# A recurrent layer in a TensorE stream: outputs placed behind the next group's gates, and the last two in full precision

## The chip, the cores and the metric

The kernel runs on one core of one Trainium2 chip, in one launch. The metric is the device time in microseconds. An execution is a run of the whole program.

## The reference, cut to what matters

The model has four layers on 256 tokens (272 with 16 meta tokens) of width 1024: an attention layer, the recurrent layer with which this case deals, and two layers of FFN, mixer and FFN. The recurrent layer, of width W = 2048:

```python
zp = einsum('btd,de->bte', z, w_in)            # u and gate, W columns each
u, gate = split(zp)
xc = conv_b + sum(up[:, tap:tap + T] * conv_w[tap] for tap in range(4))
def direction(xc, w_a, b_a, w_x, b_x, lam, reverse):
    xb = xc.reshape(B, T, 16, 128)             # 16 blocks of 128 channels
    r = sigmoid(einsum('btnd,nde->btne', xb, w_a) + b_a)
    i = sigmoid(einsum('btnd,nde->btne', xb, w_x) + b_x)
    log_a = -8.0 * r * softplus(-lam)
    a, b = exp(log_a), sqrt(-expm1(2 * log_a)) * i * xc
    return scan(h = a_t * h + b_t, reverse)
y = (direction(forward) + direction(backward)) * silu(gate)
h = h + einsum('bte,ed->btd', y, w_out)
```

All values are float32.

## The kernel before

Activations lie as [128 channels, tile, tokens]. Weights come from one stream in memory, in slabs of 128 x 1024 (512 KB), in the order of use. SyncE (SP) loads them into three buffers `raw`. ScalarE rounds a slab to its high half (`w_hi`, L452), VectorE forms the rest (`w_lo`, L888); this is a split. Both halves have a ring of six, and the splits run `LEAD` = 4 slabs ahead of TensorE. TensorE makes each product of three matmuls (`mm3`, L1431 to L1433): high by high, high weight by low activation, low weight by high activation. So 24 matmuls use up a slab. A matmul on float32 that isn't split is one line in the code and two instructions in the profile.

The recurrent layer takes its 16 blocks of channels in four groups of four. A block n = 4g + r has: an input slab (`u`, eight products of 272 columns, `from_z`); the convolution, a tap on ScalarE (L767) and three on VectorE (L1342); four gate matmuls in full precision (`lru`, L1667), whose weights POOL loads unsplit into two buffers `WL` (L401); four tanh on ScalarE (L780); an input-gate slab of 256 columns and its tanh (L791). ScalarE turns gates into decays (`decay`, L799), `tau` (L809) and, for a whole group after it, `roots` (L815, for the last group L819), with a change of the activation table before and behind. VectorE has `gated` (L1353, L1356), and `scans`: L1363, L1365, the scans L1366 and L1367, L1369, L1371. The result is split by `high` (ScalarE, L827) and `low` (VectorE, L1376) and goes with an output slab into the sums in PSUM banks 0 to 3 (`down`, eight blocks of 256 columns).

PSUM banks 4 to 7 take the tiles `u`, `lru`, `gate` in turn, by their place in `ODD_TILES` modulo 4; a tile waits for the reader of the tile four places before.

The order is written out by hand in each engine's queue. TensorE: inputs of group g, for g of 2 and 3 the output of group g - 2, gates of group g; at the end outputs 2 and 3. VectorE: four convolutions, for g of 2 and 3 four splits and `low` of group g - 2, then for each r a split, `gated` and the scans of group g - 1; at the end, for each r, split, `low` of group 2 and scans of group 3, and four splits with `low` of group 3. ScalarE goes likewise: taps (the decays, tau and roots of the group before between them), output splits and `high`, then per r gates, output gate, `decay` and `tau`. After the layer, `enter` adds the sums to the residual (L922), forms the next normalization's parts, and the first FFN's slabs follow.

## Time and profile before

| what | value |
|---|---|
| time, median of 3 runs | 1720.17 us (1717.52 to 1721.12) |
| the profiled execution's own time | 1717.52 us |
| its span | 1715.7 us |
| TensorE busy | 1598.8 us, 93% |
| VectorE busy | 1153.1 us, 67% |
| ScalarE busy | 912.1 us, 53% |
| granted clock of TensorE, mean | 0.974 of full |
| DMA | 263.67 MB, mean 154 GB/s |

The profile is one execution, times from the start of its span. The recurrent layer's first product starts at 357.98 us, and the first FFN's begins at 589.25. Durations of matmuls overlap: the distance of two starts is what one costs. A granted clock of 1.00 is 2.4 GHz, 0.50 is 1.2 GHz. A row of the timeline gives start, duration, engine, line, operation, tiles, count, and in brackets how long the engine idled before it and which instruction ended that.

### The profile page before, as it was taken

How to read it: one execution, taken by the hardware profiler on the slowest of the kernel's cores; microseconds unless marked ns; L12 is line 12 of the kernel's file. 1: busy time of each engine (PE TensorE's matmuls, PEld its weight loads, DVE VectorE, ACT ScalarE, POOL GpSimd, SP SyncE). 2: the span in 40 equal slices, each digit the busy share in tenths (PEclk: the TensorE clock that was granted, in tenths of full speed). 3: DMA queues.
4: the chain of work that ended last, by engine and by line, in shares of the span. 5: the costliest groups of instructions: out<-in, count | busy, mean ns of one | idle time of the engine just before them, and what ended most of it. 6: DMA issues, size and time to landing. Idle time of an engine off the chain costs nothing.

```text
span 1715.7 us, 32420 instructions
## 1 busy us (share of the span) xinstructions
PE 1598.8 (93%) x12554; PEld 1541.3 (90%) x12554; DVE 1153.1 (67%) x1750; ACT 912.1 (53%) x1432; POOL 44.6 (3%) x52
## 2 busy tenths in 40 slices
PE   7998797988776899999999999999999999999996
PEld 7988675987776899999999999999999899999996
DVE  4546668566686866668777766676666877776666
ACT  5453555457676454447654544455444765454443
POOL 0000000000000000000300000000000030000000
PEclk9999999989998899999999999999999999999998
DMA  5442300533442365554545565546555454546554
GB/s 194 160 159 74 97 1 1 180 126 125 135 148 84 126 203 186 186 183 136 172 148 173 167 199 185 183 159 205 186 185 188 129 175 146 176 166 199 183 183 135
DMA packets 73314, 263.67 MB, mean 154 GB/s; under 512 B 8144, under 2 KB 9680, under 8 KB 73104
## 3 DMA queue, kind: packets, MB, share of 16 engines
q1 hardware_dynamic: 71712, 256.85, 45.8%
q0 software_dynamic: 1520, 5.66, 1.0%
q8 instruction: 59, 0.97, 0.2%
q14 instruction: 23, 0.19, 0.0%
HBM read 261.43 MB, written 1.05 MB: 153 GB/s over the span
## 4 chain that ended last, share of the span: by engine, by line
PE 75%; DVE 15%; ACT 6%; issue 3%; DMA 2%; DVEq 0%; SPq 0%; ACTq 0%
PE PS L1431 22%; PE PS L1433 22%; PE PS L1432 22%; DVE w_lo L888 3%; ACT w_hi L452 1%; PE PS L1754 1%; DMA raw<-stream 1%; DVE zf L1229 1%; PE PS L1608 1%; PE PS L1442 1%; ACT work L809 1%; DVE stat L1284 1%; PE PS L1585 1%; PE PS L1586 1%; DVE zf L1280 1%
## 5 line engine op out<-in xcount | busy, mean ns | idle before, releaser
L1431 PE MATMUL PS<-YH,w_hi 128*128 128x256 f32 (+1 forms) x2876 | 831.9, 289 | 44.4 <-DVE YL L1376 31.7
L1433 PE MATMUL PS<-YH,w_lo 128*128 128x256 f32 (+1 forms) x2876 | 818.3, 285 | 0.0
L1432 PE MATMUL PS<-YL,w_hi 128*128 128x256 f32 (+1 forms) x2876 | 818.2, 285 | 0.0
L888 DVE TENSOR_TENSOR w_lo<-raw,w_hi 128x1024 fp32r<-128x1024 f32 x484 | 594.6, 1232 | 235.8 <-ACT w_hi L452 232.8
L1431 PEld LDWEIGHTS PS<-YH,w_hi 128*128 128x128 f32 x2876 | 549.3, 191 | 55.4 <-DVE YL L1376 33.8
L452 ACT ACTIVATE w_hi<-raw 128x1024 fp32r<-128x1024 f32 x484 | 508.2, 1053 | 139.9 <-PE PS L1433 87.1
L1432 PEld LDWEIGHTS PS<-YL,w_hi 128*128 128x128 f32 x2876 | 549.2, 191 | 1.9 <-issue 0.5
L1433 PEld LDWEIGHTS PS<-YH,w_lo 128*128 128x128 f32 x2876 | 550.2, 191 | 0.0
L1431 PE MATMUL PS<-hH,w_hi 128*128 128x256 f32 x832 | 233.0, 280 | 6.4 <-DVE hL L979 6.4
L1432 PE MATMUL PS<-hL,w_hi 128*128 128x256 f32 x832 | 233.0, 280 | 0.0
L1433 PE MATMUL PS<-hH,w_lo 128*128 128x256 f32 x832 | 232.9, 280 | 0.0
L1431 PEld LDWEIGHTS PS<-hH,w_hi 128*128 128x128 f32 x832 | 156.8, 188 | 7.2 <-DVE hL L979 7.2
L1432 PEld LDWEIGHTS PS<-hL,w_hi 128*128 128x128 f32 x832 | 156.5, 188 | 0.0
L1433 PEld LDWEIGHTS PS<-hH,w_lo 128*128 128x128 f32 x832 | 156.3, 188 | 0.0
L972 DVE TENSOR_TENSOR zf<-PS,work 128x256 f32<-128x256 f32 x88 | 37.2, 423 | 171.4 <-PE PS L1433 171.4
L507 ACT ACTIVATE zf<-zf 128x256 f32<-128x256 f32 x88 | 36.8, 418 | 181.7 <-DVE zf L970 181.7
L511 ACT ACTIVATE hH<-zf 128x256 fp32r<-128x256 f32 x88 | 36.6, 416 | 138.6 <-DVE zf L975 138.6
L970 DVE TENSOR_TENSOR zf<-PS,work 128x256 f32<-128x256 f32 x88 | 37.2, 423 | 33.7 <-PE PS L1433 33.7
L641 ACT ACTIVATE work<-PS 128x272 f32<-128x272 f32 (+4 forms) x61 | 23.1, 411 | 46.2 <-PE PS L1433 26.9
L1667 PE MATMUL PS<-work 128*128 128x272 f32 x128 | 35.8, 411 | 9.7 <-DVE work L1356 4.8
L975 DVE TENSOR_TENSOR zf<-zf 128x256 f32<-128x256 f32 x88 | 37.4, 425 | 5.8 <-ACT zf L507 3.3
L1667 PEld LDWEIGHTS PS<-work 128*128 128x128 f32 x128 | 22.5, 192 | 17.6 <-DVE work L1356 8.3
(288 smaller groups left out, 1377.6 us busy)
## 6 DMA issues: line engine op xcount, KB each, us to landing
raw<-stream SPq DMA_DIRECT2D x484, 512.0 KB, 4.0
work<-stream POOLq DMA_DIRECT2D x8, 512.0 KB, 4.2
X<-x SPq DMA_DIRECT2D x1, 1088.0 KB, 5.1
out<-zf SPq DMA_DIRECT2D x8, 128.0 KB, 2.0
work<-rope SPq DMA_DIRECT2D x1, 544.0 KB, 7.6
work<-levels POOLq DMA_DIRECT2D x1, 512.0 KB, 3.9
work<-inv_count POOLq DMA_DIRECT2D x1, 512.0 KB, 4.6
work<-band POOLq DMA_DIRECT2D x1, 408.0 KB, 4.6
```

The source lines that it names most:

```text
L452: act.activation(w_hi[:, s.slot, :], raw[:, s.slot % RAW, :], ACT.Copy).then_inc(hi_ready, 1)
L507: act.activation(sg[:, b, :], sg[:, b, :], ACT.Silu).then_inc(sg_ready, 1)
L511: act.activation(hH[:, b, 0:T2], hf[:, b, :], ACT.Copy).then_inc(hhi_ready, 1)
L641: act.activation(dst, PS[0:rows, 4 + j % 4, 0:width], ACT.Copy).then_inc(job_out, 1)
L888: dve.tensor_tensor(w_lo[:, s.slot, :], raw[:, s.slot % RAW, :], f32(w_hi[:, s.slot, :]), ALU.subtract).then_inc(lo_ready, 1)
L970: dve.tensor_tensor(sg[:, b, :], PS[:, 4 + b, 0:T2], rsb, ALU.mult).then_inc(ga_ready, 1)
L972: dve.tensor_tensor(hf[:, b, :], PS[:, 6 + b, 0:T2], rsb, ALU.mult).then_inc(up_ready, 1)
L975: dve.tensor_tensor(hf[:, b, :], hf[:, b, :], sg[:, b, :], ALU.mult).then_inc(hf_ready, 1)
L1431: pe.matmul(to, wh, xh, start=start, stop=False, skip_group_check=True)
L1432: pe.matmul(to, wh, xl, start=False, stop=False, skip_group_check=True)
L1433: return pe.matmul(to, wl, xh, start=False, stop=stop, skip_group_check=True)
L1667: pe.matmul(tile("lru", n, q), WL[:, n // 2 % 2, k * P:(k + 1) * P], XC[:, g % 2, r, :], start=True, stop=True, skip_group_check=True).the ...
```

## The change

- Output g - 1 is done on TensorE behind the gates of group g, for g of 1 and 2. The outputs of groups 2 and 3 come at the end, from unsplit slabs in full precision (`whole_output`): eight matmuls of 256 columns a slab, from `WL` and `GR` as they are, without `high`, `low` or split.
- POOL loads these eight slabs too. `WL` has four buffers in place of two; a wait on `whole_used` frees them. SP's ring has 40 slabs of this layer and not 48.
- VectorE and ScalarE: the scans of a group are spread over three places: set 0 at the end of the group's own phase (for group 0 behind the next convolutions), sets 1 and 2 among the next gates, set 3 among the output splits. Decay 3, tau 2 and 3 and the roots of groups 1 to 3 move from between the next taps to the end of the group's own phase.
- PSUM: inputs take banks 4 to 7, gate matmuls rotate over 4 to 6, the input gate has 7; a tile waits for the reader of the last tile in its bank.
- `high` and `low` no longer wait for a free buffer: `YH`, `YL` hold groups 0 and 1 in eight places.

```diff
@@ -54,7 +54,7 @@
...
 def o_u(g):
-    return (0, 8, 16, 28)[g]
+    return (0, 8, 20, 32)[g]
@@ -62,31 +62,45 @@
...
 def o_out(g):
-    return (20, 32, 40, 44)[g]
+    return (16, 28)[g]
...
 LRU_SLABS = 8
-O_RING = O_SLABS - LRU_SLABS
+WHOLE_SLABS = LRU_SLABS + 8
+WHOLE = 4
+O_RING = O_SLABS - WHOLE_SLABS
...
-    ring, lru = [0] * O_RING, []
+    ring, lru, out = [0] * O_RING, [], []
     for g in range(GROUPS):
...
             ring[o_gate(g) + r] = (4, 14, 28, 38)[g] + 3 * (r // 2) + r % 2
-            ring[o_out(g) + r] = (24, 44, 48, 52)[g] + r
+            if g < 2:
+                ring[o_out(g) + r] = (24, 44)[g] + r
+            else:
+                out.append((48, 52)[g - 2] + r)
         lru += [(4, 14, 28, 38)[g] + 3 * p + 2 for p in range(2)]
-    return ring, lru
+    return ring, lru + out
...
 for _g in range(GROUPS):
-    ODD_TILES += [("u", 4 * _g + _r, 0) for _r in range(4)]
+    ODD_TILES += [(4 + _r, "u", 4 * _g + _r, 0) for _r in range(4)]
     for _r in range(4):
-        ODD_TILES += [("lru", 4 * _g + _r, _q) for _q in range(4)] + [("gate", 4 * _g + _r, 0)]
+        ODD_TILES += [(4 + (4 * (4 * _g + _r) + _q) % 3, "lru", 4 * _g + _r, _q) for _q in range(4)] + [(7, "gate", 4 * _g + _r, 0)]
+def odd_place(kind, n, q=0):
+    banks = [t[0] for t in ODD_TILES]
+    at = [t[1:] for t in ODD_TILES].index((kind, n, q))
+    older = [i for i in range(at) if banks[i] == banks[at]]
+    return banks[at], ODD_TILES[older[-1]][1:] if older else None
@@ -227,7 +241,7 @@
...
         GR, GS = part(2, 4, T2), part(4, T2)
-        WL = part(2, SLAB)
+        WL = part(WHOLE, SLAB)
         HS = zf[:, 0:2, :]
@@ -272,7 +286,7 @@
...
         sp_d, sp_a = sem("sp_d"), sem("sp_a")
-        lru_landed = [sem(f"lru_landed{i}") for i in range(2)]
+        whole_landed, whole_used = [sem(f"whole_landed{i}") for i in range(WHOLE)], sem("whole_used")
         tap_done, xc_ready, lru_done, lru_out = sem("tap_done"), sem("xc_ready"), sem("lru_done"), sem("lru_out")
@@ -328,14 +342,12 @@
...
-        RING_SOURCE, LRU_SOURCE = odd_source()
+        RING_SOURCE, WHOLE_SOURCE = odd_source()
         def odd_bank(kind, n, q=0):
-            return 4 + ODD_TILES.index((kind, n, q)) % 4
+            return odd_place(kind, n, q)[0]
         J_KS, J_QS, J_VS, J_Q, J_K, J_V, J_G, J_ODD = 6, 8, 16, 19, 31, 39, 45, 61
         UNITS = [("pe", 0), ("sk", 0)] + [(kind, j) for j in range(4) for kind in ("mq", "mk", "sq")]
@@ -357,18 +369,19 @@
...
                 sp.dma_start(m, mats[:, i, :]).then_inc(c_loaded, 16)
-            for n in range(RAW, E_SLABS + O_RING):
+            first = -(-(E_SLABS + O_RING) // RAW)
+            for n in range(RAW, first * RAW):
                 sp.wait_ge(lo_ready, n - RAW + 1)
-                source = n if n < E_SLABS else E_SLABS + RING_SOURCE[n - E_SLABS]
+                source = n if n < E_SLABS else E_SLABS + RING_SOURCE[n - E_SLABS] if n < E_SLABS + O_RING else n + WHOLE_SLABS
                 sp.dma_start(raw[:, n % RAW, :], stream[source]).then_inc(landed[n % RAW], 16)
-            with sp.Fori((E_SLABS + O_RING) // RAW, (slabs - LRU_SLABS) // RAW) as turn:
+            with sp.Fori(first, (slabs - WHOLE_SLABS) // RAW) as turn:
                 for s in range(RAW):
...
                     sp.wait_ge(lo_ready, turn * RAW + s - RAW + 1)
-                    sp.dma_start(raw[:, s, :], stream[turn * RAW + s + LRU_SLABS]).then_inc(landed[s], 16)
-            for n in range((slabs - LRU_SLABS) // RAW * RAW, slabs - LRU_SLABS):
+                    sp.dma_start(raw[:, s, :], stream[turn * RAW + s + WHOLE_SLABS]).then_inc(landed[s], 16)
+            for n in range((slabs - WHOLE_SLABS) // RAW * RAW, slabs - WHOLE_SLABS):
                 sp.wait_ge(lo_ready, n - RAW + 1)
-                sp.dma_start(raw[:, n % RAW, :], stream[n + LRU_SLABS]).then_inc(landed[n % RAW], 16)
+                sp.dma_start(raw[:, n % RAW, :], stream[n + WHOLE_SLABS]).then_inc(landed[n % RAW], 16)
             for c in range(DC):
@@ -394,11 +407,13 @@
...
             pool.wait_ge(x_ready, 4)
-            for i in range(LRU_SLABS):
-                if i >= 2:
-                    pool.wait_ge(lru_done, 8 * (i - 1))
-                pool.dma_start(WL[:, i % 2, :], stream[E_SLABS + LRU_SOURCE[i]]).then_inc(lru_landed[i % 2], 16)
+            for i in range(WHOLE_SLABS):
+                if i >= WHOLE + LRU_SLABS:
+                    pool.wait_ge(whole_used, i - WHOLE - LRU_SLABS + 1)
+                elif i >= WHOLE:
+                    pool.wait_ge(lru_done, 8 * (i - WHOLE + 1))
+                pool.dma_start(WL[:, i % WHOLE, :], stream[E_SLABS + WHOLE_SOURCE[i]]).then_inc(whole_landed[i % WHOLE], 16)
@@ -821,41 +836,41 @@
...
                     act.wait_ge(oy_ready, n + 1)
-                    if g >= 2:
-                        act.wait_ge(w_used, odd(o_out(g - 2) + r).n + 1)
-                    act.activation(YH[:, 8 + n % 8, 0:T2], GR[:, g % 2, r, :], ACT.Copy).then_inc(oyhi_ready, 1)
+                    act.activation(YH[:, 8 + n, 0:T2], GR[:, g % 2, r, :], ACT.Copy).then_inc(oyhi_ready, 1)
...
                         tap(g, r)
-                        if g and r == 0:
-                            decay(g - 1, 3)
-                            tau(g - 1, 2)
-                            tau(g - 1, 3)
-                        if g and r == 1:
-                            roots(g - 1)
-                    if g >= 2:
-                        for r in range(4):
-                            split(odd(o_out(g - 2) + r + LEAD))
-                            high(g - 2, r)
+                        if g == 1 and r == 0:
+                            decay(0, 3)
+                            tau(0, 2)
+                            tau(0, 3)
+                        if g == 1 and r == 1:
+                            roots(0)
                     for r in range(4):
...
                             decay(g, r - 1)
-                            if r > 1:
-                                tau(g, r - 2)
-                decay(LAST, 3)
-                tau(LAST, 2)
-                tau(LAST, 3)
-                roots(LAST)
-                for r in range(4):
-                    split(odd(o_out(LAST - 1) + r + LEAD))
-                    high(LAST - 1, r)
-                for r in range(4):
-                    split(odd(o_out(LAST) + r + LEAD))
-                    high(LAST, r)
+                        if r > 1:
+                            tau(g, r - 2)
+                            if 0 < g < LAST:
+                                high(g - 1, r - 2)
+                    if g:
+                        if g < LAST:
+                            split(odd(o_out(g - 1) + LEAD))
+                        decay(g, 3)
+                        tau(g, 2)
+                        if g < LAST:
+                            split(odd(o_out(g - 1) + 1 + LEAD))
+                        tau(g, 3)
+                        if g < LAST:
+                            high(g - 1, 2)
+                            split(odd(o_out(g - 1) + 2 + LEAD))
+                            high(g - 1, 3)
+                        roots(g)
+                        if g < LAST:
+                            split(odd(o_out(g - 1) + 3 + LEAD))
@@ -916,6 +931,8 @@
...
                     dve.wait_ge(sums_ready, 3 * n + j + 1)
+                elif s is None:
+                    dve.wait_ge(whole_used, WHOLE_SLABS - LRU_SLABS)
                 else:
@@ -1373,28 +1390,33 @@
...
                     dve.wait_ge(oyhi_ready, n + 1)
-                    dve.tensor_tensor(YL[:, 8 + n % 8, 0:T2], GR[:, g % 2, r, :], f32(YH[:, 8 + n % 8, 0:T2]),
+                    dve.tensor_tensor(YL[:, 8 + n, 0:T2], GR[:, g % 2, r, :], f32(YH[:, 8 + n, 0:T2]),
                                       ALU.subtract).then_inc(oylo_ready, 1)
...
                         conv(g, r)
-                    if g >= 2:
-                        for r in range(4):
-                            split(odd(o_out(g - 2) + r + LEAD))
-                            low(g - 2, r)
+                    if g == 1:
+                        scans(0, 0)
                     for r in range(4):
...
                         gated(g, r)
-                        if g:
+                        if g and r in (1, 2):
                             scans(g - 1, r)
+                    if 0 < g < LAST:
+                        low(g - 1, 0)
+                        low(g - 1, 1)
+                        split(odd(o_out(g - 1) + LEAD))
+                        scans(g - 1, 3)
+                        split(odd(o_out(g - 1) + 1 + LEAD))
+                        low(g - 1, 2)
+                        split(odd(o_out(g - 1) + 2 + LEAD))
+                        low(g - 1, 3)
+                        split(odd(o_out(g - 1) + 3 + LEAD))
+                        scans(g, 0)
+                scans(LAST - 1, 3)
                 for r in range(4):
-                    split(odd(o_out(LAST - 1) + r + LEAD))
-                    low(LAST - 1, r)
                     scans(LAST, r)
-                for r in range(4):
-                    split(odd(o_out(LAST) + r + LEAD))
-                    low(LAST, r)
@@ -1407,7 +1429,7 @@
...
             for lay in range(LAYERS):
-                enter(lay * 3, lay * 3 + 1, layer_slab(lay, -1), 0.5, lay * C_LAYER + C2 + C_F1)
+                enter(lay * 3, lay * 3 + 1, layer_slab(lay, -1) if lay else None, 0.5, lay * C_LAYER + C2 + C_F1)
                 ffn(layer_slab(lay, K_FFN[0]), lay * 2 * FF, lay * 3)
@@ -1636,39 +1658,54 @@
...
-                    at = ODD_TILES.index((kind, n, q))
-                    if at >= 4:
-                        was, m, k = ODD_TILES[at - 4]
+                    bank, older = odd_place(kind, n, q)
+                    if older:
+                        was, m, k = older
                         if was == "u":
...
                             pe.wait_ge(lru_out, 4 * m + k + 1)
-                    return PS[:, odd_bank(kind, n, q), 0:width]
+                    return PS[:, bank, 0:width]
...
                         pe.wait_ge(oylo_ready, n + 1)
-                        down(odd(o_out(g) + r), YH[:, 8 + n % 8, 0:T2], YL[:, 8 + n % 8, 0:T2], n == 0, n == 15)
+                        down(odd(o_out(g) + r), YH[:, 8 + n, 0:T2], YL[:, 8 + n, 0:T2], n == 0, False)
+                def whole_output(g):
+                    for r in range(4):
+                        n = 4 * g + r
+                        i = LRU_SLABS + n - 8
+                        pe.wait_ge(whole_landed[i % WHOLE], 16 * (i // WHOLE + 1))
+                        pe.wait_ge(oy_ready, n + 1)
+                        for m in range(DC):
+                            last = pe.matmul(PS[:, m // 2, (m % 2) * T2:(m % 2 + 1) * T2], WL[:, i % WHOLE, m * P:(m + 1) * P],
+                                             GR[:, g % 2, r, :], start=False, stop=n == 15, skip_group_check=True)
+                            if n == 15 and m in (1, 3, 5):
+                                last.then_inc(sums_ready, 1)
+                        last.then_inc(whole_used, 1)
...
                         from_z(odd(o_u(g) + r), tile("u", 4 * g + r), 1 if g == r == 0 else None, T1)
-                    if g >= 2:
-                        output(g - 2)
                     for r in range(4):
                         n = 4 * g + r
-                        pe.wait_ge(lru_landed[n // 2 % 2], 16 * (n // 4 + 1))
+                        i = n // 2
+                        pe.wait_ge(whole_landed[i % WHOLE], 16 * (i // WHOLE + 1))
                         pe.wait_ge(xc_ready, n + 1)
...
                             k = 4 * (r % 2) + q
-                            pe.matmul(tile("lru", n, q), WL[:, n // 2 % 2, k * P:(k + 1) * P], XC[:, g % 2, r, :],
+                            pe.matmul(tile("lru", n, q), WL[:, i % WHOLE, k * P:(k + 1) * P], XC[:, g % 2, r, :],
                                       start=True, stop=True, skip_group_check=True).then_inc(lru_done, 1)
                         from_z(odd(o_gate(g) + r), tile("gate", n, 0, T2), None, T2, XO)
-                output(LAST - 1)
-                output(LAST)
+                    if 0 < g < LAST:
+                        output(g - 1)
+                whole_output(LAST - 1)
+                whole_output(LAST)
 
```

## Rows read from the trace of the kernel before

**Rows 1.** Windows by stage: us, busy (instructions) per engine, clock, DMA, GB/s.

```profile
412.90:469.40 56.50, 46.83 (x322) 43.72 (x320) 39.27 (x60) 34.94 (x58) 1.06 (x2) 0.91 0.41 134
469.40:524.30 54.90, 45.00 (x320) 41.82 (x320) 39.17 (x60) 35.56 (x60) 1.05 (x2) 0.94 0.42 135
524.30:589.20 64.90, 46.75 (x312) 43.34 (x312) 50.54 (x80) 34.87 (x63) 0.00 (x0) 0.84 0.30 98
```

**Rows 2.** List of waits, 358 to 589 us: total, times, longest.

```profile
PE PS L1431 <- DVE YL L1376: 31.7, 6, 11.7
...
PE PS L1667 <- DVE work L1356: 4.8, 6, 0.9
```

**Rows 3.** Timeline of TensorE: start, duration, instruction, idle before and releaser.

```profile
453.67 0.58 PE L1431 MATMUL PS<-YH,w_hi 128*128 128x256 f32 x1 [7.67 <-DVE YL L1376]
...
479.51 0.72 PE L1667 MATMUL PS<-work 128*128 128x272 f32 x2 [0.83 <-DVE work L1356]
...
555.56 0.58 PE L1431 MATMUL PS<-YH,w_hi 128*128 128x256 f32 x1 [11.66 <-DVE YL L1376]
...
565.80 0.39 PE L1431 MATMUL PS<-YH,w_hi 128*128 128x256 f32 x1 [2.03 <-DVE YL L1376]
```

**Rows 4.** Timeline of TensorE without waits: gate pair, then four input slabs.

```profile
378.38 2.00 PE L1667 MATMUL PS<-work 128*128 128x272 f32 x8
380.01 0.48 PE L1431 MATMUL PS<-YH,w_hi 128*128 128x256 f32 x1
...
383.02 1.99 PE L1667 MATMUL PS<-work 128*128 128x272 f32 x8
...
488.85 0.29 PE L1431 MATMUL PS<-YH,w_hi 128*128 128x272 f32 x1
...
500.83 0.29 PE L1433 MATMUL PS<-YH,w_lo 128*128 128x272 f32 x1
```

**Rows 5.** Timeline of VectorE: one scan set, a split and the gating.

```profile
473.62 0.72 DVE L1363 SCALAR_TENSOR_TENSOR work<-work 128x544 f32<-128x544 f32 x1
...
477.27 1.22 DVE L888 TENSOR_TENSOR w_lo<-raw,w_hi 128x1024 fp32r<-128x1024 f32 x1
478.41 0.72 DVE L1353 SCALAR_TENSOR_TENSOR work<-work 128x544 f32<-128x544 f32 x1
479.04 0.41 DVE L1356 SCALAR_TENSOR_TENSOR work<-work,PS 128x256 f32<-128x256 f32 x1
```

**Rows 6.** Timeline of ScalarE: tap, table load, root; output gate, decay, tau.

```profile
401.79 0.58 ACT L767 ACTIVATE work<-PS,C 128x272 f32<-128x272 f32 x1
402.39 1.28 ACT L815 ACT_TABLE_LOAD   x1
403.68 2.02 ACT L815 ACTIVATE work<-work 128x2176 f32<-128x2176 f32 x1
...
483.08 0.38 ACT L791 ACTIVATE work<-PS 128x256 f32<-128x256 f32 x1 [1.37 <-PE PS L1433]
483.36 1.11 ACT L799 ACTIVATE work<-work,sp 128x272 f32<-128x272 f32 x2
484.37 1.11 ACT L809 ACTIVATE work<-work,sp 128x272 f32<-128x272 f32 x2
```

**Rows 7.** Windows of one microsecond, columns as in the first group.

```profile
413.00:414.00 1.00, 1.00 (x6) 0.88 (x5) 0.00 (x0) 0.44 (x2) 0.00 (x0) 0.50 0.36 143
...
567.00:568.00 1.00, 1.00 (x7) 1.00 (x6) 0.97 (x3) 0.00 (x0) 0.00 (x0) 0.50 0.84 336
...
570.00:571.00 1.00, 0.50 (x5) 0.29 (x3) 1.00 (x3) 0.47 (x1) 0.00 (x0) 0.99 0.00 0
```

**Rows 8.** Timeline of TensorE at the fourth gate matmul of tile 4.

```profile
412.25 1.27 PE L1667 MATMUL PS<-work 128*128 128x272 f32 x2 [1.50 <-DVE work L1342]
```

**Rows 9.** Timeline of ScalarE: the four roots of group 3.

```profile
550.67 2.29 ACT L819 ACTIVATE work<-work 128x544 f32<-128x544 f32 x4
```

**Rows 10.** DMA issues: count, KB each, median us from issue to landing.

```profile
work<-stream POOLq DMA_DIRECT2D x8, 512.0 KB, 4.2
```

## The prediction

> **What bounds the kernel now.** I read the windows by stage first. In the recurrent layer TensorE works 46.8 of 56.5 us, 45.0 of 54.9 and 46.8 of 64.9 in three stretches, at a granted clock of 0.84 to 0.94 of full; in the last VectorE is busier, 50.5 [rows 1]. The reader sees there a layer in which no engine is full. The list of waits says who ends TensorE's idle time: the low half of a gated output (L1376), 31.7 us in six waits of matmuls, 11.7 the longest (and about as much again put on weight loads); 4.8 us are put on VectorE's L1356 [rows 2]. TensorE's timeline gives the places: 7.67 us before output 0 (and as much again before output 1), 11.66 before output 2, then 2.03 inside the last eight output slabs (and 2.12 once more), and 0.83 before a fourth gate matmul, of which there are five alike [rows 3]. So the layer is bound by order: outputs stand where their inputs are not ready, and in the tail each slab waits for its scans, a split and a low half on VectorE.
>
> **Unit costs.** One pair of gates and input gate goes from 378.38 to 383.02, 4.64 us without a wait [rows 4]. Of these the split slab (24 matmuls of 256 columns) has 383.02 less 380.01, 3.01, of which 0.18 is still the matmul before (the pitch of the rest is 0.118): 2.83. The four full-precision matmuls of 272 columns are then 1.81, 0.453 each; at 256 columns 0.426, so an output slab of eight in full precision is 3.41 us. An input slab: 95 pitches in 11.98 us [rows 4], 0.126 each, 3.03. VectorE: a scan set goes from 473.62 to 477.27, 3.65 us; a split's pitch is 1.14, the first gating operation's 0.63; the second has 0.41 less the 0.08 by which these rows overlap, 0.33, and a low half of the same shape is taken at 0.34 [rows 5]. ScalarE: output gate 0.28 by pitch, decay 1.01 for two instructions (tau, of the same shape, as much, and a gate tanh 0.5), a tap 0.58, a table load 1.28 [rows 6].
>
> **The change, part by part.** I take TensorE's work from the gate of tile 4 on (before it the order is as now) and add the waits that the other two queues leave. A group's cycle (gates, output of the group before, inputs of the next) is 4 x 4.64 + 4 x 2.83 + 4 x 3.03 = 42.0 us. The waits:
> - *Banks.* Gates rotate over three banks, the input gate has the fourth. The fourth gate matmul no longer waits for L1356 of the tile before, but for ScalarE's first tanh of its own tile. In the third tile that stands behind output gate and decay (0.28 + 1.01 + 0.5 and 0.2 for hand-overs, less the 1.36 of three matmuls: 0.65); in the fourth behind tau and a high half too (1.0 + 0.3 more: 1.9); in the first behind the last tap and the table load (0.58 + 1.28 + 0.5, less 1.36: 1.0). Bounds for the three together: nothing, where VectorE is late anyway, to 5.
> - *Output behind the gates.* The first low half follows the last gating: 1.2 us after the gates. The third slab's low half is queued on VectorE behind two low halves, a split that waits for ScalarE's high half, a scan set and another split. From the gates' end: 3.7 to the first of these splits' start, then 1.14 + 3.65 + 1.14 + 0.34 = 10.0 us; the first wait and two slabs take 1.2 + 5.66. So 3.2 us. Bounds: 0, since [rows 3] has slabs that follow without a wait, and 7.67, the wait of now.
> - *Scans.* Sets 1 and 2 lie beside the gates, 3 between the output's splits, 0 at the end of it. VectorE's sum for a cycle is 4 x (1.14 + 1.60) for convolutions, 4 x 3.65, 4 x (1.14 + 0.96), 4 x 1.48 for the output: 39.9 us. It is under 42.0 and doesn't become the bound, by only 2.
> - *Clock.* After the wait of 2.03 us the clock is at 0.50 in the slice from 567 and at 0.99 in that from 570 [rows 7]: 3 us or a little more at half speed; I take 1.7 us lost. I saw no such fall after the waits of 0.83. So I charge the 3.2 us wait 1.8 and each 1.9 us wait half of 1.7. At tile 4 the clock is at 0.50 [rows 7] and stays so: 1.8, in place of the 1.1 us by which the gating would be late there (scan set 0 of group 0 is put ahead of it).
>
> Group 1, gate 4 to gate 8: 42.0 + 0.65 + 1.9 + 1.0 + 1.2 + 3.2 + 1.8 + 1.8 = 53.5; now it is the first stretch of [rows 1], 56.5. Group 2, without the slow start: 51.7; now 54.9, the second stretch. Gate 4 starts at 412.25 and not 0.68 later: now the fourth gate matmul waits till then for the fourth convolution [rows 8], after only the gate does. Together 6.9 us won.
>
> - *The tail.* Group 3's gates cost about what they do now (3 more pairs, and 0.65 + 1.9 for the waits of 0.83 and the like): now TensorE idles from 555.56 less 11.66, 543.90 [rows 3], and a matmul's row reaches 0.16 beyond its pitch, so they end at 543.7; the last stretch ends with the layer at 589.2 [rows 1]: 45.5 us. After, eight slabs of 3.41 are 27.3: TensorE has 8 x 0.58 = 4.7 us more work than with split slabs, VectorE and ScalarE lose eight splits and halves. Let T be the gates' end. Output 2's last set is done at T + 4.5 and used at T + 10.2. For group 3 ScalarE has decay, tau, decay, tau, tau, a load and a first root, as now, where the first of the four roots ends 0.6 after 550.67 [rows 9]: T + 7.6. Sets end at T + 11.2, 14.9, 18.5, 22.2; the slabs want them at T + 13.6, 17.1, 20.5, 23.9. With 1.7 us to spare they are hidden; were this cover gone, each us of delay beyond it costs one. The tail can't be under 22.2 + 3.4 = 25.6. Won: 18.2.
> - *DMAs.* POOL issues eight slabs of 512 KB more, SP eight less. A slab lands in 4.2 us [rows 10]; with four buffers one comes free three slabs, 10.2 us, ahead of its use, so it is hidden; a landing of 12 us would cost 2 for each of the last four. The two loads that now go first have nothing waiting behind them. levels and inv_count stand behind the last slab on POOL, but wait for the layer's end anyway.
> - *Hand-over to the FFN.* It is VectorE's own chain from the second column pair on; the last slab's extra 0.58 is in the 27.3.
>
> Sum: 6.9 + 18.2 less 3 x 0.85 is 22.6, say 23 us. The profiled execution took 1717.52 around a span of 1715.7, so 1694.5 for one like it. The median of the runs is 1720.17, 2.65 above it: I forecast 1697.
>
> **A rule weighed.** On ScalarE the switch to square roots took 1.28 us, 402.39 to 403.67, and the next instruction began at 403.68 [rows 6]. The Trainium skill (ScalarE: Activation LUTs, What ACT_TABLE_LOAD costs) says that a switch also drains for some 1.38 us. By that, an estimate from its figure, two cycles would be 1.4 us dearer each and the sum 20. The trace doesn't agree for this switch, so the sum goes by the row.
>
> **Rivals.**
> 1. *Only the tail pays.* The third slab's wait is near 7 us, because its low half sits behind a scan set and ScalarE's chain per tile is longer. For it: VectorE has only 2 us to spare in a cycle. Against: it also loses no time there to the 7 us stalls that it has now. Won 18.2 less up to 2: 1703. Chance 0.13.
> 2. *Shorter waits, no clock loss.* 2 x 1.8, 2.6 and a part of the tanh waits come back: 1689. For it: 0.83 us waits cost no clock. Chance 0.10.
> 3. *Slower: the clock doesn't come back.* Four waits now follow each other within 20 us. If after them the clock stayed at 0.50 through the output and the first input slab (14.4 us of work, doubled, less the 1.8 counted: 12.6) in two cycles, and through half of the full-precision stretch (13.7), it would cost 38.9 against 22.6: 1736. It decides from some 23 us of work at 0.50 on, beyond what is counted. For it: the low clock around tile 4. Against: after the 2.03 us wait it was back within 4 us [rows 7]. Chance 0.03.
> 4. *The change doesn't do what it says:* the last eight slabs still wait, for a landing or a set, and keep half of the 18 us: 1706. Chance 0.05.
> 5. *A switch holds up the first tanh by a second 1.28* [rows 6]: 2 x 1.3 dearer, 1700. Nothing in the rows speaks for it. Chance 0.01. It is the skill's rule above, put in this kernel's numbers.
>
> **How the numbers follow.** The forecast has 0.68, its own bounds being 1690 to 1704 (the sum of the waits at half or one and a half times, and the runs' spread). The range takes in rivals 1, 2, 4 and 5: 1687 to 1707. A difference below 0.2%, 3.4 us, can't be told from none. All cases but rival 3 are faster by more; 0.03 is left for waits that eat all.
>
> **What would show it.** In the trace after: no wait over 4 us before an output; one of about 3 us before the third slab of outputs 0 and 1, ended by a low half; fourth gate matmuls that wait for L780's successor; a last stretch of 64 full-precision matmuls (128 instructions) in 27 us without a wait at clock 1; a layer some 23 us shorter and the rest as it was. Wrong would be: waits for scans or landings in that stretch, clock 0.5 in it, or a cycle of over 55 us.

## The result and the profile after

The changed kernel took 1692.48 us (median of 4 runs, 1690.17 to 1695.36), the kernel before 1720.55 beside it (4 runs): the ratio is 0.9841, interval 0.9819 to 0.9863. That is 28 us less between the medians and 23.3 between the two profiled executions (1694.27 and 1717.52). The forecast was 1697, a gain of 23.

In the profiled execution the recurrent layer, from its first product to the FFN's first, takes 563.80 - 357.07 = 206.73 us, where it took 231.27. Outside it the span differs little: the layer starts 0.9 us earlier, and behind it the rest takes 2.3 us longer, with one short fall of the clock (0.50 from 1368.4 to 1371.8 us), in a part that the change doesn't touch.

"Gate n" stands for the first product of block n's input-gate slab, "tile n" for the block's matmuls, and a cycle is the time from gate 4 to gate 8 or from gate 8 to gate 12. The two cycles of the changed kernel (columns as in [rows 1]):

```profile
412.48:465.93 53.45, 44.99 (x321) 41.95 (x321) 43.30 (x66) 35.69 (x59) 1.06 (x2) 0.97 0.44 144
465.93:516.88 50.95, 43.35 (x322) 40.56 (x321) 39.72 (x60) 35.88 (x60) 1.06 (x2) 1.00 0.46 143
```

Against [rows 1] the two cycles went from 56.5 and 54.9 us to 53.45 and 50.95. VectorE, at 39.72 of 50.95 us, is still not the bound. The list of TensorE's waits, 358 to 564 us (waiting for, total, times, longest):

```profile
PE PS L1702 <- ACT work L795: 11.9, 11, 1.8
PE PS L1453 <- DVE YL L1393: 8.3, 4, 2.9
PE PS L1702 <- DVE work L1359: 2.9, 1, 2.9
PE PS L1453 <- DVE work L1373: 0.9, 1, 0.9
```

The low half (now L1393) ends 8.3 us of waits in four places, where it ended 31.7 in six [rows 2]. What is new is 11.9 us in eleven waits for a gate's tanh (L795), most of them the price of three banks for the gate products. Before, the gating ended 4.8 us of waits and a tanh 2.0, in three. TensorE's timeline, group 1 and its output:

```profile
409.74 3.08 PE L1702 MATMUL PS<-work 128*128 128x272 f32 x6 [2.88 <-DVE work L1359]
...
418.36 0.39 PE L1453 MATMUL PS<-YH,w_hi 128*128 128x256 f32 x1 [0.89 <-DVE work L1373]
...
430.00 0.73 PE L1702 MATMUL PS<-work 128*128 128x272 f32 x2 [1.79 <-ACT work L795]
...
434.83 0.39 PE L1453 MATMUL PS<-YH,w_hi 128*128 128x256 f32 x1 [1.26 <-DVE YL L1393]
...
443.69 0.58 PE L1453 MATMUL PS<-YH,w_hi 128*128 128x256 f32 x1 [2.89 <-DVE YL L1393]
...
465.57 0.72 PE L1702 MATMUL PS<-work 128*128 128x272 f32 x2 [1.15 <-ACT work L795]
...
536.36 27.79 PE L1686 MATMUL PS<-work 128*128 128x256 f32 x128
```

The waits of 7.67 and 11.66 us [rows 3] are gone. In their place stand 1.26 us before an output and 2.89 before its third slab. The last row is the whole tail: 64 full-precision products, two instructions each, without a gap. The FFN's first matmul follows at 563.80, so the tail from the gates' end takes 27.44 us, where it took 45.5.

Why the third slab waits 2.89 us, on VectorE's timeline of the same execution:

```profile
438.43 0.72 DVE L1380 SCALAR_TENSOR_TENSOR work<-work 128x544 f32<-128x544 f32 x1
...
441.74 0.42 DVE L1388 TENSOR_TENSOR work<-work,zf 128x256 f32<-128x256 f32 x1
442.08 1.22 DVE L903 TENSOR_TENSOR w_lo<-raw,w_hi 128x1024 fp32r<-128x1024 f32 x1
443.22 0.42 DVE L1393 TENSOR_TENSOR YL<-work,YH 128x256 fp32r<-128x256 f32 x1
```

The low half at 443.22, which the slab at 443.69 needs, is queued behind a scan set (438.43 to 442.08) and a split.

### The profile page after: what moved, and what is told of

Read it like the earlier page. It is cut to its first block, busy times and chain, and to the rows that moved or that the text cites. A ratio compares the mean times of both kernels' runs of the same rounds, so it can differ in the third digit from the quotient of the medians.

```text
span 1692.5 us, 32254 instructions
## 1 busy us (share of the span) xinstructions
PE 1594.2 (94%) x12490; PEld 1536.2 (91%) x12490; DVE 1141.7 (67%) x1734; ACT 902.7 (53%) x1416; POOL 48.4 (3%) x60
## 4 chain that ended last, share of the span: by engine, by line
PE 79%; DVE 11%; ACT 5%; issue 2%; DMA 2%; DVEq 0%; SPq 0%; ACTq 0%
PE PS L1453 23%; PE PS L1455 23%; PE PS L1454 23%; DVE w_lo L903 2%; PE PS L1686 2%; PE PS L1791 1%; DMA raw<-stream 1%; ACT w_hi L467 1%; DVE zf L1246 1%; PE PS L1630 1%; PE PS L1702 1%; PE PS L1464 1%; PE PS L1607 1%; DVE stat L1301 1%; ACT work L814 1%
## 5 line engine op out<-in xcount | busy, mean ns | idle before, releaser
L1453 PE MATMUL PS<-YH,w_hi 128*128 128x256 f32 (+1 forms) x2812 | 809.8, 288 | 19.8 <-DVE YL L1393 8.3
L1455 PE MATMUL PS<-YH,w_lo 128*128 128x256 f32 (+1 forms) x2812 | 796.5, 283 | 0.0
L1454 PE MATMUL PS<-YL,w_hi 128*128 128x256 f32 (+1 forms) x2812 | 796.4, 283 | 0.0
L903 DVE TENSOR_TENSOR w_lo<-raw,w_hi 128x1024 fp32r<-128x1024 f32 x476 | 584.0, 1231 | 213.5 <-ACT w_hi L467 210.0
L1453 PEld LDWEIGHTS PS<-YH,w_hi 128*128 128x128 f32 x2812 | 533.2, 190 | 27.5 <-issue 9.8
L467 ACT ACTIVATE w_hi<-raw 128x1024 fp32r<-128x1024 f32 x476 | 499.3, 1052 | 104.2 <-PE PS L1455 57.6
L1454 PEld LDWEIGHTS PS<-YL,w_hi 128*128 128x128 f32 x2812 | 533.0, 190 | 2.1 <-issue 0.5
L1455 PEld LDWEIGHTS PS<-YH,w_lo 128*128 128x128 f32 x2812 | 534.1, 190 | 0.0
L1702 PE MATMUL PS<-work 128*128 128x272 f32 x128 | 36.6, 415 | 14.7 <-ACT work L795 11.9
```

Source lines behind the costliest of these rows:

```text
L467: act.activation(w_hi[:, s.slot, :], raw[:, s.slot % RAW, :], ACT.Copy).then_inc(hi_ready, 1)
L903: dve.tensor_tensor(w_lo[:, s.slot, :], raw[:, s.slot % RAW, :], f32(w_hi[:, s.slot, :]), ALU.subtract).then_inc(lo_ready, 1)
L1453: pe.matmul(to, wh, xh, start=start, stop=False, skip_group_check=True)
L1454: pe.matmul(to, wh, xl, start=False, stop=False, skip_group_check=True)
L1455: return pe.matmul(to, wl, xh, start=False, stop=stop, skip_group_check=True)
L1702: pe.matmul(tile("lru", n, q), WL[:, i % WHOLE, k * P:(k + 1) * P], XC[:, g % 2, r, :], start=True, stop=True, skip_group_check=True).then ...
```

## Experiments

None of these kernels leaves part of the computation out. "Layer" is the time from the layer's first product to the FFN's first, read from TensorE's timeline of each run's one profiled execution. Ratios are to the kernel before, on the same chip. The changed kernel, e1 to e4, e5 to e8 and e9 to e11 are four such comparisons; across them medians compare less well than ratios.

| kernel | median us | ratio | interval | layer us | cycles us |
|---|---|---|---|---|---|
| before | 1718.6 to 1720.6 | 1 | | 231.3 | 56.5, 54.9 |
| changed | 1692.48 | 0.9841 | 0.9819 to 0.9863 | 206.7 | 53.5, 51.0 |
| e1 order only | 1713.85 | 0.9968 | 0.9955 to 0.9982 | 228.0 | 55.0, 52.5 |
| e2 tail only | 1703.00 | 0.9903 | 0.9886 to 0.9920 | 216.1 | 57.0, 56.7 |
| e3 two buffers | 1698.39 | 0.9882 | 0.9866 to 0.9899 | 212.8 | 55.0, 52.4 |
| e4 low half first | 1692.57 | 0.9846 | 0.9830 to 0.9863 | 206.4 | 52.3, 50.5 |
| e5 changed again | 1695.32 | 0.9853 | 0.9830 to 0.9876 | 209.9 | 55.1, 52.4 |
| e6 all unsplit | 1686.42 | 0.9812 | 0.9796 to 0.9828 | 200.4 | 49.6, 48.5 |
| e7 old banks | 1690.30 | 0.9836 | 0.9819 to 0.9852 | 205.6 | 53.3, 51.3 |
| e8 roots in one | 1695.68 | 0.9868 | 0.9851 to 0.9884 | 205.4 | 52.1, 50.9 |
| e9 unsplit, roots later | 1688.67 | 0.9828 | 0.9815 to 0.9842 | 200.9 | 50.0, 48.5 |
| e10 = e9, old banks | 1683.34 | 0.9794 | 0.9781 to 0.9808 | 196.8 | 49.4, 47.3 |
| e11 = e6 again | 1689.85 | 0.9833 | 0.9820 to 0.9846 | 200.7 | 49.9, 48.4 |

### The two halves of the change

e1: outputs 2 and 3 are split again, the order of the other two stays.

```diff
-    return (16, 28)[g]
+    return (16, 28, 40, 44)[g]
-WHOLE_SLABS = LRU_SLABS + 8
+WHOLE_SLABS = LRU_SLABS
-                whole_output(LAST - 1)
-                whole_output(LAST)
+                output(LAST - 1)
+                output(LAST)
```

> The changed kernel with outputs 2 and 3 split again as before (SP brings their slabs, high and low halves, three matmuls each); the order of groups, scans and banks is the new one. The layer, from its first product to the FFN's first, took 231.3 us before and 206.8 after. My theory (two separate gains, 7 us from the cycles and 18 from the tail): cycles as after, tail of 45 us as before, layer 224 to 226, time 6 to 8 us under the kernel before. Rival (the new order also frees the tail, because outputs 2's sets are done early): layer 215 or less.

e2: the old order of outputs, scans and roots, with the whole outputs at the end.

```diff
-    return (0, 8, 20, 32)[g]
+    return (0, 8, 16, 28)[g]
-    return (16, 28)[g]
+    return (20, 32)[g]
...
-                    if 0 < g < LAST:
-                        output(g - 1)
```

> The changed kernel with the old order of groups and scans (output g - 2 before the gates of g, sets beside the gates), outputs 2 and 3 in full precision from unsplit slabs. Theory: cycles near 56 and 55 us again with waits of about 7.7 us before outputs 0 and 1, a tail of 27.3 to 28 us, layer 213 to 215, time 17 to 19 us under the kernel before. Rival (full precision alone doesn't shorten the tail, since the scan sets of group 3 or set 3 of group 2 come late in the old order): a wait in the last 64 matmuls and a tail of over 30.

Measured: 5.5 us of gain for the order alone ((1 - 0.9968) x 1718.8), 16.7 for the tail alone, in the layer 3.3 and 15.2. The order alone falls short of its 6 to 8 us, and its layer of 228.0 misses the 224 to 226. TensorE's waits in e1's tail are those of [rows 3]:

```profile
552.93 0.58 PE L1461 MATMUL PS<-YH,w_hi 128*128 128x256 f32 x1 [11.67 <-DVE YL L1396]
563.19 0.38 PE L1461 MATMUL PS<-YH,w_hi 128*128 128x256 f32 x1 [2.03 <-DVE YL L1396]
...
573.44 0.38 PE L1461 MATMUL PS<-YH,w_hi 128*128 128x256 f32 x1 [2.12 <-DVE YL L1396]
```

And in e2 the wait before output 0 is that of before, while the tail is one row, as in the changed kernel:

```profile
456.14 0.58 PE L1434 MATMUL PS<-YH,w_hi 128*128 128x256 f32 x1 [7.69 <-DVE YL L1384]
...
548.44 27.79 PE L1667 MATMUL PS<-work 128*128 128x256 f32 x128
```

So each half does its own work: the unsplit slabs remove the tail's waits without help from the order, and the order removes the two waits of 7.7 us without help from the tail. Their layers' gains, 18.5 us together, are 6 less than the 24.5 of the changed kernel, and that is no effect of one half on the other. From gate 12 on the layer is 18.0 us shorter in e2 (46.93 us for 64.91) and in the changed kernel (46.92). What e2 loses lies ahead of it: its cycles, 57.0 and 56.7 us, are longer than those of before with the same waits before the outputs, some 1.4 us of it by the clock (an estimate: behind the second wait it is at 0.50 for 5.9 us, where it was for 3.2), the rest with the three banks. And e1's cycles, 55.0 and 52.5, are those that the changed kernel has in e5 below, with the clock low behind every third-slab wait. e10 below prices the banks.

### Four buffers

e3:

```diff
-WHOLE = 4
+WHOLE = 2
```

> The changed kernel with two WL buffers in place of four. Theory (landing of 4.2 us is hidden by four buffers, not by two): in the tail a slab can land only some 5 us after the slab two before is used, against 3.4 us of work, so about 1.6 us of wait at each second of the last six slabs, 4 to 6 us in all, layer 211 to 212; nothing in the cycles. Rival (loads were not on the path at all and two would do): no wait before the last 64 matmuls' pairs, layer 207.

Measured: 2.9 us longer in the layer than e5 (212.8 against 209.9, cycles alike); by the medians it is 3.1, by the ratios 5.0, across two comparisons. In the tail of e3 TensorE waits for loads:

```profile
547.26 7.32 PE L1686 MATMUL PS<-work 128*128 128x256 f32 x32 [0.67 <-DMA work<-stream]
555.12 7.33 PE L1686 MATMUL PS<-work 128*128 128x256 f32 x32 [0.54 <-DMA work<-stream]
562.89 7.33 PE L1686 MATMUL PS<-work 128*128 128x256 f32 x32 [0.45 <-DMA work<-stream]
```

With two buffers a slab's load starts when the last but one is done, and 3.4 us of work cover most of a landing, but not all. Four cover it: no such row exists in the tail of the changed kernel. The three waits are 1.66 us of the 2.9; the rest goes where the product before a wait no longer overlaps with the next. The mechanism was right, the size under the 4 to 6 us expected.

### The wait before the third slab

e4: the third low half stands ahead of scan set 3 (VectorE), with its high half to match (ScalarE).

```diff
                         split(odd(o_out(g - 1) + LEAD))
-                        scans(g - 1, 3)
                         split(odd(o_out(g - 1) + 1 + LEAD))
                         low(g - 1, 2)
+                        scans(g - 1, 3)
+                        low(g - 1, 3)
                         split(odd(o_out(g - 1) + 2 + LEAD))
-                        low(g - 1, 3)
```

> The changed kernel with the third low half of outputs 0 and 1 (and its high half) put ahead of scan set 3, the two splits ahead of it; the fourth low half right behind the set. Theory (the 2.89 us wait is the set's place in VectorE's queue, and the clock's fall behind it is its result): that wait goes, one of about 1 us comes before the fourth slab, the clock stays at 1.00 through output and inputs, each cycle is 2.5 to 3 us shorter, layer 201 to 202. Rival (VectorE is the bound behind it, so the time comes back as later convolutions): the wait moves to the gates, layer 205 to 207.

Measured: 1692.57 us, 2.8 less than e5 and no less than the changed kernel at first; the ratios, 0.9846 against 0.9853 and 0.9841, don't differ. The wait went, and part of it came back elsewhere:

```profile
447.55 0.38 PE L1452 MATMUL PS<-YH,w_hi 128*128 128x256 f32 x1 [0.93 <-DVE YL L1392]
...
464.48 1.61 PE L1701 MATMUL PS<-work 128*128 128x272 f32 x6 [1.73 <-DVE work L1358]
...
517.98 0.58 PE L1452 MATMUL PS<-YH,w_hi 128*128 128x256 f32 x1 [1.21 <-DVE work L1358]
```

The third slab no longer waits, the fourth does for 0.93 us, and at the next group's gates a convolution is late by 1.73. The rival was right about the place and the layer (206.4). Of its reason, that VectorE is the bound, one half holds: VectorE works without a gap up to that convolution, but ahead of it stands this:

```profile
451.35 1.23 DVE L902 TENSOR_TENSOR w_lo<-raw,w_hi 128x1024 fp32r<-128x1024 f32 x1 [2.72 <-ACT w_hi L467]
```

It idled 2.72 us for the high half of a split, which ScalarE makes behind the group's roots. Ordering that split ahead of the roots was not tried. The clock stayed at 1.00 through both outputs and all inputs, as expected; it fell one group later, at 517.53 us, among waits of 0.81 and 1.21 us. Beside e8 below, whose clock stayed at 1.00 too, the second cycle is 0.4 us shorter and the first no shorter: moving the low half is worth little beyond the clock.

### The changed kernel once more

e5 is the changed kernel without an edit.

> The changed kernel itself once more, beside the next three. In the four runs so far, the slow clock at tile 4 lasted 2.8 us less in the changed kernel's profile than in the others. Theory (luck of that execution): cycles of 55.0 and 52.5 us, as in the run with two buffers up to its tail, layer 209 to 211, time 25 to 28 us under the kernel before. Rival (it belongs to this kernel): layer 207 again.

Measured: cycles of 55.1 and 52.4 us, a layer of 209.9, where the first profile had 206.7, and 23.5 us of gain by the medians (25 by the ratio). The waits are the same in both, to 0.02 us, but for the 0.89 at tile 5, which only the first has. What differs is the clock behind them, in windows of TensorE's work behind the first 2.89 us wait. In e5:

```profile
447.00:449.00 2.00, 2.00 (x10) 2.00 (x11) 1.18 (x2) 1.99 (x2) 0.00 (x0) 0.50 0.81 233
```

And in e8, after a wait of 2.90 us at the same place:

```profile
444.00:445.00 1.00, 1.00 (x11) 1.00 (x10) 0.33 (x1) 1.00 (x1) 0.00 (x0) 1.00 0.72 291
```

Twelve such stretches of 144 matmuls, behind a wait of 2.5 to 2.9 us, are in the changed kernel, e1, e3, e5, e7 and e8. In three of them the clock stays at 1.00 and the stretch takes 17.94 to 17.97 us. In nine it falls to 0.50, for 19.35 to 20.65 us. The fall costs 1.4 to 2.7 us when it comes, 1.4 as a mean over all twelve. The longer low clock at tile 4, which I had in view, is only 0.2 of the 3.2 us between the two profiles; the two third-slab waits have the rest.

### The tail's roots

e8: the last group's roots in one instruction, as for the other groups.

```diff
-                    if g < LAST:
-                        act.activation(LW[:, g % 2], LW[:, g % 2], ACT.Sqrt, scale=0.25).then_inc(sw_ready, 1)
-                    else:
-                        for r in range(4):
-                            lw = LW[:, g % 2, 2 * r:2 * r + 2, :]
-                            act.activation(lw, lw, ACT.Sqrt, scale=0.25).then_inc(sw_ready, 1)
+                    act.activation(LW[:, g % 2], LW[:, g % 2], ACT.Sqrt, scale=0.25).then_inc(sw_ready, 1)
```

> The changed kernel with the roots of group 3 in one operation and not four, so that the first set of group 3 starts some 1.4 us later. Theory (there are 1.7 us to spare between the sets and the full-precision slabs): no wait in the last 64 matmuls, tail 27.6, no change. Rival (no such slack): a wait of about 1 us or more in the tail.

Measured: the tail is the same single row. First VectorE's first and last instruction of the sets in e8, then those in the changed kernel:

```profile
543.15 0.73 DVE L1375 SCALAR_TENSOR_TENSOR work<-work 128x544 f32<-128x544 f32 x1 [4.27 <-ACT work L829]
...
557.43 0.42 DVE L1383 TENSOR_TENSOR work<-work,zf 128x256 f32<-128x256 f32 x1
```

```profile
543.99 0.73 DVE L1380 SCALAR_TENSOR_TENSOR work<-work 128x544 f32<-128x544 f32 x1 [2.92 <-ACT work L834]
...
558.27 0.42 DVE L1388 TENSOR_TENSOR work<-work,zf 128x256 f32<-128x256 f32 x1
```

From the gates' end (534.16 and 536.36) the last set ends after 23.7 us in e8 and after 22.3 in the changed kernel. The last slab is wanted at 24.0 (27.44 less 3.43). So the cover had 1.7 us to spare, and one root for all takes 1.35 of them: the split into four roots gives nothing as long as the slabs take 3.43 us each. The time, 1695.68, is that of e5. The profile here is of the fastest of four executions, the one in e5 of the slowest.

### The banks

e7: gate products and input gate over four banks in turn, as before, in the new order.

```diff
-        ODD_TILES += [(4 + (4 * (4 * _g + _r) + _q) % 3, "lru", 4 * _g + _r, _q) for _q in range(4)] + [(7, "gate", 4 * _g + _r, 0)]
+        ODD_TILES += [(4 + (5 * _r + _q) % 4, "lru", 4 * _g + _r, _q) for _q in range(4)] + [(4 + (5 * _r + 4) % 4, "gate", 4 * _g + _r, 0)]
```

> The changed kernel with the four banks in turn as before. Theory (the new banks' waits for the first tanh, 0.5, 1.8 and 1.1 us a group, are dearer than the old waits for the gating, 0.8 each): waits of 0.8 or less at the fourth gate matmuls, each cycle about 1 us shorter, layer 1 to 4 us shorter than the changed kernel's. Rival (with the scans moved, the gating comes later than the tanh, so the rotation is needed): waits of over 1.5 us put on L1373's successor, layer 2 us longer or more.

Measured: 1690.3 us, a layer of 205.6 with the clock low behind both third-slab waits, 4.3 us shorter than e5, in which it fell behind both too (1.2 of the 4.3 is a shorter first fall: 19.45 us against 20.65 for the 144 matmuls). By the ratios alone (0.9836 against 0.9841 and 0.9853) that isn't told apart. It was taken up again without the third-slab waits, below.

### Beyond the change

e6: all four outputs in full precision from unsplit slabs, in the new order, with no high or low halves and no output splits.

```diff
-WHOLE_SLABS = LRU_SLABS + 8
+WHOLE_SLABS = LRU_SLABS + 16
...
                     if 0 < g < LAST:
-                        output(g - 1)
+                        whole_output(g - 1)
```

> All four outputs in full precision from unsplit slabs: no split, high or low half in this layer's outputs; POOL loads 24 slabs. Theory (waits before outputs are splits and low halves in VectorE's queue; TensorE's extra 0.58 us a slab is cheaper): no wait before outputs 0 and 1, waits only at the fourth gate matmuls, cycles 47 to 48.5 us, layer 198 to 201, time 33 to 38 us under the kernel before. Rival (convolutions become the bound, as they began to with the low half put first): waits for L1342's successor before the gates, layer 204 or more.

e9 is e6 with this edit, e10 is e9 with the four banks of e7, e11 is e6 once more:

```diff
-                        if g == 1 and r == 1:
+                        if g == 1 and r == 3:
                             roots(0)
```

> All four outputs in full precision from unsplit slabs, and the roots of group 0 issued behind the four convolution taps of group 1, where they stood behind the second. Theory (tile 4 starts late because taps and convolutions 6 and 7 stand in ScalarE's queue behind 1.28 us of table load and 2.0 of roots): taps and convolutions 6 and 7 come 3.3 us earlier, the wait of 2.89 us of tile 4 goes, but the gate's tanh still starts only after roots and a table load (409.5 in the run of all outputs unsplit), so a wait of 0.7 to 2 us on ScalarE stands in its place; the 0.97 us wait of the convolution sum behind the first scan goes too. From the first gate slab of tile 4 to that of tile 8 then 47 to 48.5 us (49.6 there), 1 to 2.5 us less in all, 1684 to 1686 us, ratio 0.980 to 0.981. Rival: ScalarE's whole stretch is the bound, and the layer's length stays within 0.5 us.

> As the kernel before it in this list, with the gate products in four banks in turn as in the kernel of before. Theory (the waits at a tile's gates are ScalarE's tanh time, and banks only choose which matmul waits): 1.4 us shorter waits in a group, and within 1.5 us of the run with the new banks, 1682 to 1686 us. Rival: with the outputs no longer waiting, the banks are what stands at the fourth gate, and the four banks are worth 1.4 us in each of three groups and 1 in the first, 5 us in all: 1680 us.

> All four outputs in full precision from unsplit slabs, the run of the first time once more, beside the other two on one chip: 1686.4 us and ratio 0.981, as then, within 2 us. If the gain of 6 us over the changed kernel was chance it comes back nearer to 1692.

Measured: e6 has cycles of 49.6 and 48.5 us and a layer of 200.4. Its output of four slabs is one row again, 13.97 us without a wait, where the changed kernel has 11.3 us of work and 4.15 of waits:

```profile
432.57 13.97 PE L1667 MATMUL PS<-work 128*128 128x256 f32 x64
```

Beside e5 in the same comparison e6 is 8.9 us faster (1695.32 less 1686.42), and the intervals of the two ratios don't meet. Its gain over the kernel before, 32.4 us, is a little under the 33 to 38 expected. e11, the same kernel in another comparison, took 1689.85, 3.4 more than e6 and outside the 2 us that I had allowed: by the ratios (0.9812 and 0.9833 against 0.9841 and 0.9853) the gain lies between 1.4 and 7 us. The layers are surer. With the clock at 1.00 from 360 us to the layer's end, e6 has 200.4 and e8 205.4: 5 us for the waits. e5, at 209.9, lost another 4.2 to the clock behind its third-slab waits, which e6 and e11 don't have.

e9 gained nothing over e11 (200.9 against 200.7): my theory fell, and its rival held. The third tap came at 403.97 us and ScalarE was free again at 405.5, but the fourth tap waits for its own input slab on TensorE and starts at 406.95. Roots and table load then stand whole in front of the gate's first tanh. ScalarE's timeline, and TensorE's wait:

```profile
407.55 1.28 ACT L831 ACT_TABLE_LOAD   x1
408.84 2.02 ACT L831 ACTIVATE work<-work 128x2176 f32<-128x2176 f32 x1
410.87 1.28 ACT L796 ACT_TABLE_LOAD   x1
412.17 1.25 ACT L796 ACTIVATE work<-PS,C 128x272 f32<-128x272 f32 x3
```

```profile
412.71 0.86 PE L1683 MATMUL PS<-work 128*128 128x272 f32 x2 [3.27 <-ACT work L796]
```

e10 is the fastest kernel of the study: 1683.34 us (5 runs, 1681.52 to 1686.05), ratio 0.9794, interval 0.9781 to 0.9808. It differs from e9 by the banks alone and is 5.3 us faster by the medians, 4.1 in the layer, on the same chip; the intervals of the two ratios don't meet. I had expected 1.5 us at most, and the rival 5. Against e11 it is 6.5 us and 3.9 in the layer. TensorE's waits in group 2's gates, in e10 and then in e11:

```profile
461.29 0.73 PE L1683 MATMUL PS<-work 128*128 128x272 f32 x2 [0.96 <-DVE work L1348]
...
476.19 0.73 PE L1683 MATMUL PS<-work 128*128 128x272 f32 x2 [0.37 <-DVE work L1362]
...
477.31 0.38 PE L1434 MATMUL PS<-YH,w_hi 128*128 128x256 f32 x1 [0.39 <-ACT work L796]
```

```profile
463.56 0.73 PE L1683 MATMUL PS<-work 128*128 128x272 f32 x2 [1.15 <-ACT work L796]
...
473.61 0.72 PE L1683 MATMUL PS<-work 128*128 128x272 f32 x2 [0.48 <-ACT work L796]
...
480.03 0.72 PE L1683 MATMUL PS<-work 128*128 128x272 f32 x2 [1.49 <-ACT work L796]
```

1.72 us against 3.12, and the cycle 47.3 against 48.4. So the three-bank rotation is a loss inside the change: with four banks in turn the products wait mostly for gating and convolutions on VectorE, which come sooner than ScalarE's tanh.

## Why the prediction was right, and where its sizes were off

The mechanism held. The time, 1692.48 us, lies inside the range; it is 4.5 us under the forecast, between it and rival 2. That it came so near is in part luck: one term was too large and two were missing. Step by step:

- *The tail, 18.2 us.* The changed kernel has 27.44 us for 27.3, and the gain is 18.1. The time to spare at the last slab came out at 1.7 us, as worked out. e2 shows it alone: 16.7 us by the ratios, with the price of three banks inside. Rival 4 (slabs that still wait) is out.
- *No wait over 4 us before an output.* It is 1.26 and 2.89 us, for 1.2 and 3.2 forecast, with the cause that was named: the third low half behind a scan set and a split. Rival 1 (7 us there, only the tail pays) is out.
- *Tanh waits.* 1.15, 0.48 and 1.79 us in a cycle, for 1.0, 0.65 and 1.9.
- *The work of a cycle, 42.0 us.* TensorE is busy 43.35 us in the second cycle. The distances between starts leave out that the last matmul before each wait doesn't overlap with the next; five waits make most of the 1.35 us. Two cycles make 2.6 us more.
- *The start, 0.68 us earlier.* It is not: gate 4 comes 55.41 us after the layer's first product, where it came 54.95 after. I took the layer before tile 4 to be as now, and left out that the three banks hold for group 0 too. There the products wait 1.09, 0.47 and 1.48 us for a tanh, where they waited twice 0.90, and group 1's first input product starts 37.06 us after the layer's first product, not 35.92. In e7 and e10, with four banks, it starts at 35.95 and 35.92. That is the whole loss of 1.1 us against the forecast. The low clock at tile 4 has no part in it: in e8, at 1.00, the gate waits for the fourth convolution and comes after 55.47 us all the same. A wait of group 0 in the changed kernel, and e8's gate 4:

```profile
390.77 0.72 PE L1702 MATMUL PS<-work 128*128 128x272 f32 x2 [1.48 <-ACT work L795]
```

```profile
411.70 0.39 PE L1448 MATMUL PS<-YH,w_hi 128*128 128x256 f32 x1 [1.10 <-DVE work L1354]
```

- *The clock: the step that was mis-sized.* I charged 1.8 for each third-slab wait, 1.8 at tile 4 and 0.85 for each 1.9 us wait, 7.95 in all. The stretch behind a 1.79 us wait takes 3.16 to 3.21 us for 24 matmuls in the changed kernel, e1, e5 and e8, which is full speed: these cost nothing. Tile 4 costs 1.24 us over a pair's 4.64 (412.48 to 418.36) at a clock of 1.00, because scan set 0 now stands ahead of the gating; in e5, at a low clock, it costs 1.44. The clock itself took 1.4 us in the changed kernel's profile, 4.4 in e5's (2.7, 1.5 and 0.2), none in e8's.

Put into the forecast's layer, 231.3 - 22.6 = 208.7: 2.6 more for work, 0.8 less for waits, 1.1 more at the start, 5.3 less for clock and tile 4 (7.95 less 1.4 and 1.24), 0.1 more for the tail is 206.4, and 206.7 was measured. For e5, with more falls of the clock, the same sum gives 209.4 for 209.9. So errors of opposite sign met: 3.7 us of work and of banks in group 0 that I had put at nothing, and 5.3 us too much for the clock and tile 4.

Rival 2 (shorter waits, no clock loss) was right about the clock in e8's profile and wrong about the waits. Rival 3 (the clock stays low) is out: in every profile of the new order the clock was back at 1.00 within 7 us of the wait's end (the longest is e10's at tile 4, from 410.50 to 417.06). Rival 5, a drain beside the table load as the Trainium skill has it (ScalarE: Activation LUTs, What ACT_TABLE_LOAD costs), is not borne out: in e9's rows above the next instruction follows each load by 0.01 to 0.02 us, and the second load starts 0.01 us after the root ahead of it has ended.

What stays open: the medians gained 28 us in the first comparison and 23 to 25 in the second (e5, ratio 0.9853), with intervals of 4 us each way. Over the eight executions of the changed kernel the time goes with the mean granted clock: 1690 to 1692 us at 0.988 to 0.984, 1694 and 1695 at 0.983 and 0.981, 1698 twice at 0.979. So the spread goes with the clock. Which waits it fell behind is known for the two profiled executions only, and why it falls behind one wait and not behind its like stays open; no run was made to steer it.

## What to carry to other kernels

Where the end of a stage is a chain of split, half and product per slab, the product that takes TensorE longer (3.43 us a slab against 2.83) but needs no preparation can be faster: count what stands in front of each slab, not the busy time of its matmuls. When an order is changed together with a rotation of buffers, price the rotation by itself, also in the stretches where the order stays; here it cost some 4 us of what the order won, and taking it back (e10) is a one-line edit. A wait shortened by moving one instruction ahead of another comes back at the next reader, where the queue has no time to spare in that stretch, whatever its mean; so look who now stands behind, and what the queue itself waits for (e4).

## What the runs showed of the hardware

- The granted clock's fall is not fixed by the wait ahead of it. The same idle of 2.9 us at the same place was followed by 0.50 in nine stretches and by 1.00 in three; at tile 4, after 2.9 us, in the profiles with three banks and the roots in their first place, by 0.50 in seven and by 1.00 in two (e6, e8). After a single idle time of 1.79 us it never fell, in twelve cases; after the kernel before's 2.03 it did [rows 7], and in e4 it did once among idle times of 0.81 and 1.21 us within 4 us of each other.
- The full-precision products ran at nearly one price everywhere: 64 of 256 columns in 27.44 us, 0.429 each, and 32 in 13.62 us in e6, 0.426 each, with the clock at 1.00. A stretch of 27 us that needs one 512 KB slab in 3.43 us was fed by POOL's queue (landing 4.2 us by the median) without a wait with four buffers.
